# A mixture-of-experts kernel: six expert weight slots instead of four, and weight rows of 24 KB instead of three pieces of 8 KB

## The reference, cut to what matters

```python
scores = jax.nn.sigmoid(tf @ router_w)
_, idx = lax.top_k(scores + router_bias, TOP_K)            # 8 of 64
gate = ROUTED_SCALE * gate / jnp.sum(gate, -1, keepdims=True)
...
def expert_block(acc, blk):                                # a block: the slots of one expert
    tok, g, e = blk
    xb = t_ext[tok]
    hb = jax.nn.silu(xb @ w1[e]) * (xb @ w3[e])
    return acc.at[tok].add((hb @ w2[e]) * g[:, None]), None
...
shared = (jax.nn.silu(tf @ sw1) * (tf @ sw3)) @ sw2
return acc[:n_tok] + shared
```

## Time and profile before

| | |
|---|---|
| median of 3 runs | 2488.39 us (2487.3 to 2493.26) |
| the profiled execution | 2497.42 us |
| its span | 2495.5 us |
| mean granted clock of TensorE | 0.888 |
| PE busy | 1998.0 us (80%) |
| DMA, mean over the span | 241 GB/s |

### The profile page before, as it was taken

One profiled execution on the slowest core, in us unless ns is written; L12 is line 12 of the kernel. 1 busy time (PEld: TensorE's weight loads), 2 busy tenths in 40 slices (PEclk: granted clock), 3 DMA queues, 4 the chain that ended last, 5 costly groups with the idle time before them and its releaser, 6 DMA issues. The chain is left out here.

```text
span 2495.5 us, 31783 instructions
## 1 busy us (share of the span) xinstructions
PE 1998.0 (80%) x10528; PEld 1022.9 (41%) x10529; DVE 856.1 (34%) x1752; ACT 236.5 (9%) x517; POOL 678.0 (27%) x961
## 2 busy tenths in 40 slices
PE   4795679955778988899998986859768887787795
PEld 0343433333355544455454433324455444443442
DVE  0005710077545222233232353654352222222224
ACT  0102101122020000000000011011110000000001
POOL 0000000022003554466565400000005444344340
PEclk8896689967877999899999988979879999899898
DMA  9300067100224899988999565130247999999964
GB/s 390 160 1 1 5 243 270 59 1 1 89 82 168 346 410 402 402 343 337 372 357 399 239 286 227 52 135 34 89 192 303 399 415 399 396 394 392 402 277 171
DMA packets 99962, 601.47 MB, mean 241 GB/s; under 512 B 23200, under 2 KB 23435, under 8 KB 40444
## 3 DMA queue, kind: packets, MB, share of 16 engines
q1 hardware_dynamic: 66012, 516.78, 51.4%
q0 software_dynamic: 33888, 83.86, 9.0%
HBM read 590.50 MB, written 51.92 MB: 257 GB/s over the span
## 5 line engine op out<-in xcount | busy, mean ns | idle before, releaser
L1593 PE MATMUL bank<-moe_w,blk_xT 128*64 128x256 f32 x5632 | 701.1, 405 | 0.0
L1593 PEld LDWEIGHTS bank<-moe_w,blk_xT 128*64 128x64 f32 x5632 | 413.7, 146 | 230.6 <-issue 50.5
L1521 POOL DMA_INDIRECT blk_came<-v_tokens,blk_gidx x352 | 362.1, 1029 | 185.9 <-issue 180.5
L1667 DVE STREAM_TRANSPOSE blk_xT<-blk_came 128x512 f32<-128x512 f32 x176 | 125.3, 712 | 614.2 <-PE bank L1593 597.2
L1604 PE MATMUL bank<-moe_w,blk_hT 128*64 128x512 f32 x1408 | 332.0, 592 | 1.5 <-DVE blk_hT L1679 1.5
L450 PE MATMUL bank<-w_in_ring,xt 128*128 128x512 f32 x544 | 243.1, 607 | 12.5 <-DMA w_in_ring<-in_odd_w_in 9.7
L1537 POOL DMA_INDIRECT y_rows<-blk_y,blk_sidx x176 | 179.3, 1019 | 97.3 <-issue 48.4
L1686 DVE COPY blk_y<-bank 128x512 f32<-128x512 f32 x176 | 121.7, 692 | 149.3 <-PE bank L1604 149.3
L450 PEld LDWEIGHTS bank<-w_in_ring,xt 128*128 128x128 f32 x544 | 104.8, 194 | 148.5 <-issue 138.4
L1586 PE MATMUL bank<-base,blk_hidden 128*128 128x128 f32 x176 | 58.9, 335 | 132.6 <-DMA moe_w<-in_experts 130.5
L1650 ACT ACTIVATE blk_silu<-bank 128x128 f32<-128x128 f32 x174 | 48.2, 277 | 1112.2 <-PE bank L1593 1112.2
(11 more groups left out here) (381 smaller groups left out, 1652.5 us busy)
## 6 DMA issues: line engine op xcount, KB each, us to landing
moe_w<-in_experts SPq DMA_DIRECT2D x128, 3072.0 KB
ada_ring<-in_ada_w SPq DMA_DIRECT2D x12, 2048.0 KB, 16.4
w_out<-in_ada_w POOLq DMA_DIRECT2D x12, 2048.0 KB, 7.7
moe_w<-y_rows SPq DMA_DIRECT2D x24, 1024.0 KB, 18.9
w_in_ring<-in_even_w_in SPq DMA_DIRECT2D x8, 2048.0 KB, 11.7
w_in_ring<-in_odd_w_in SPq DMA_DIRECT2D x7, 2048.0 KB, 12.5
blk_came<-v_tokens,blk_gidx POOLq DMA_INDIRECT x352
w_out<-in_even_w_out SPq DMA_DIRECT2D x1, 4096.0 KB, 12.5
```

The source lines that it names most:

```text
L1521: pool.indirect_dma_start(came[:, q, u], None, v_quarters, bass.IndirectOffsetOnAxis(ap=gidx[q][:, u:u + 1], axis=0), bounds_check=4 * n_t ...
L1593: last = nc.tensor.matmul(g.bank[1][64 * h:64 * h + 64, 0:HID], xT[:, k], w[:, s, (2 * k + h) * HID:(2 * k + h + 1) * HID], start=k == 0, ...
L1667: nc.vector.transpose(xT[:].rearrange("p k (u t) -> p u k t", u=2), came[:, q].rearrange("p u (k t) -> p u k t", k=KT)).then_inc(xt_ready, 1)
```

## The change

`SLOTS` is 6 and `PIECE` is the whole row, so a weight load is 128 runs of 24 KB. The room for two more slots (48 KB a partition) comes from scratch tiles that now lie elsewhere: the router's tables in slots not yet loaded, `came` for three of four blocks in `ada_rows`, `y`, `silu`, `hidden`, `hT` and one half of `sh_hidden` in `xt`, and the rows, `z` and `sh_down` of the last stage in `w`. Three things move with that. `sh_down` is loaded at the start of `expert_residual_stage` instead of in `routing_stage`. `ada_columns_stage(g, 1)` runs in the even layer, ahead of `hgrn_stage`, since `ada_rows` is overwritten afterwards. `routing_stage` loads experts 0 to 3; expert 4 is loaded at the start of `blocks_stage` without a wait, expert 5 after `shared_up`. As 64 is no multiple of 6, the loops take ten turns of six, the first written out, and four more experts are written out behind. The ring of the last stage has 13 places instead of 10.

```diff
-SLOTS = 4
+SLOTS = 6
+WHOLE_TURNS, LAST_EXPERTS = EXPERTS // SLOTS, EXPERTS % SLOTS
...
-PIECE = 2 * D
+PIECE = WEXP
...
-    RING = 10
+    RING = 13
...
+                sp.dma_start(sh_down, g.dram["experts"][l * (EXPERTS + 1), 0, :, W13:WEXP]).then_inc(sh_down_loaded, 16)
                 for u in range(nt * PAIRS):
...
-                for s in range(SLOTS - 1):
+                for s in range(SLOTS - 2):
                     load_expert(sp, r["w"][:, s], experts[1 + s]).then_inc(r["expert_loaded"][s], 16)
-                load_expert(sp, r["sh_down"], experts[0, W13 // PIECE:]).then_inc(r["sh_down_loaded"], 16)
...
-        came, xT = sb("came", [P, DEPTH, 2, D // 4]), sb("xT", [P, KT, SB])
+        came = [g.ada_rows[:, q] for q in range(3)] + [sb("came", [P, D // 2])[:]]
...
+                load_expert(sp, w[:, SLOTS - 2], experts[SLOTS - 2]).then_inc(loaded[SLOTS - 2], 16)
                 sp.wait_ge(sh_up_done, 1)
                 load_expert(sp, w[:, SLOTS - 1], experts[SLOTS - 1]).then_inc(loaded[SLOTS - 1], 16)
-
-                with sp.Fori(1, EXPERTS // SLOTS) as turn:
+                with sp.Fori(1, WHOLE_TURNS) as turn:
                     for s in range(SLOTS):
...
+                        load(turn, s)
+                for s in range(LAST_EXPERTS):
+                    load(WHOLE_TURNS, s)
...
-                pool.memset(came[:], 0.0).then_inc(came_zeroed, 1)
-                pool.wait_ge(came_zeroed, 1)
+                for x in came:
+                    pool.memset(x, 0.0).then_inc(came_zeroed, 1)
+                pool.wait_ge(came_zeroed, DEPTH)
...
-                with pe.Fori(1, EXPERTS // SLOTS) as turns:
+                with pe.Fori(1, WHOLE_TURNS) as turns:
                     for s in range(SLOTS):
                         expert(turns, s)
+                for s in range(LAST_EXPERTS):
+                    expert(WHOLE_TURNS, s)
...
+            ada_columns_stage(g, 1)
             hgrn_stage(g, work, {"q": q[:], "v": v, "f": (ff[:], fb[:]), "y": y})
```

More of the change, by code:

```diff
@@ L1105, in expert_residual_stage @@
     diag = room[:, RING * 2 * D:RING * 2 * D + nt * BY_PE * P].rearrange("p (u c) -> p u c", c=P)
+    rest = room[:, RING * 2 * D + nt * BY_PE * P:]
+    sh_down, sh_down_loaded = rest[:, 0:2 * D], new_sem(g, "sh_down_loaded")
+    ln, z = (rest[:, (2 + 2 * i) * D:(4 + 2 * i) * D].rearrange("p (a d) -> p a d", a=2) for i in range(2))
     with ExitStack() as ctx:
         sb = lambda n, shape: ctx.enter_context(nc.sbuf_tensor(f"xln_{n}{l}", shape, F32))
-        ln, z, stats, mv = sb("rows", [P, 2, D]), sb("z", [P, 2, D]), sb("stats", [P, 2, 2, 6]), sb("mv", [P, 4, 4])
+        stats, mv = sb("stats", [P, 2, 2, 6]), sb("mv", [P, 4, 4])
         marks = {}
@@ L1134, in _ @@
                         for half in range(2):
-                            nc.tensor.matmul(g.bank[2 * n + half][:], r["sh_hidden"][:, m, n * P:(n + 1) * P],
-                                             r["sh_down"][:, m * D + half * 512:m * D + (half + 1) * 512], start=m == 0, stop=False)
+                            nc.tensor.matmul(g.bank[2 * n + half][:], r["sh_hidden"][m][:, n * P:(n + 1) * P],
+                                             sh_down[:, m * D + half * 512:m * D + (half + 1) * 512], start=m == 0, stop=False)
                     for k in range(BY_PE):
@@ L1311, in routing_stage @@
         chosen_f, lin, blk, slot, val = (sb(n, [P, nt, TOPK]) for n in ("chosen_f", "lin", "blk", "slot", "val"))
[L1312 to L1314 removed]
+        free, at = r["w"][:, SLOTS - 2], 0
+        tables = []
+        for shape in ((nt, TOPK, EXPERTS), (1, TOPK, EXPERTS), (2, TOPK, SB), (2, TOPK, NB)):
+            size = math.prod(shape)
+            tables.append(free[:, at:at + size].rearrange("p (a b c) -> p a b c", a=shape[0], b=shape[1]))
+            at += size
+        onehot, prod, in_slot, in_block = tables
+        prod = prod[:, 0]
+        rb, nblk, incl, start, odd = (free[:, at + i * EXPERTS:at + (i + 1) * EXPERTS] for i in range(5))
         ecol, val0 = sb("ecol", [P, 2]), sb("val0", [P, 1])
[L1316 to L1318 removed]
         flat = lambda t: t[:].rearrange("p n e -> p (n e)")
@@ L1339, in _ @@
                     dve.wait_ge(squashed, n + 1)
[L1340 removed]
+                    link(nc.vector.tensor_tensor(pick[:, n], sig[:, n], rb, ALU.add))
                     link(nc.vector.max(top[:, n], pick[:, n]))
@@ L1438, in _ @@
                 for u in range(3):
-                    last = nc.tensor.matmul(g.bank[2][:, u * NB:(u + 1) * NB], g.spread[:, u], listing[:], start=True, stop=True)
+                    last = nc.tensor.matmul(g.bank[2][:, u * NB:(u + 1) * NB], g.spread[:, u], listing, start=True, stop=True)
                 last.then_inc(laid, 1)
@@ L1585, in turn_hidden @@
                     pe.wait_ge(hidden_done, b + 1)
-                    nc.tensor.transpose(g.bank[2][:, 0:P], hidden[:], g.ident).then_inc(hid_turned, 1)
+                    nc.tensor.transpose(g.bank[2][:, 0:P], hidden, g.ident).then_inc(hid_turned, 1)
                 def up_project(b, s):
@@ L2180, in odd_layer @@
     nc = g.nc
-    ada_columns_stage(g, 1)
     allt, lat = list(range(NT)), [2, 3]
```

111 lines of the change are left out of this document (59 added, 52 removed).

## The result

The changed kernel takes 2523.7 us (median of 4 runs, 2521.53 to 2533.84), the kernel before on the same chip 2487.85 (2487.09 to 2493.26). The ratio is 1.0147, 95% interval 1.0116 to 1.0178: slower, where 2441 was forecast, and outside the range. The profiled execution has a span of 2532.0 us, 36.5 more than before.

A forecast was written before the change was run, and what follows sets the result against it. Layer 0 was taken as bound by DMA, then PE, then DMA again, layer 1 by saturated DMA. Terms of -33 (layer 0), -21 (layer 1), +5 and +2 (costs) gave -47 us: 2441 us from 2488.39, range 2412 to 2476.

The forecast's parts named there:

- the term for the rows: Weight loads in both layers: longer rows take 0.12 us off a load, 3 us in layer 0 and 7 in layer 1.
- rival 1: In the expert blocks, long weight rows hold up the gathers: a tail of 27 us, 2468 us; chance 0.13.
- The head start: Expert loads issued earlier: a lead of two loads, 16 us, in layer 0; 1.6 loads, 13.9 us, in layer 1.
- the slots: Two more weight slots: 7 us off the later waits in layer 0, nothing by itself in layer 1.
- beyond the waits: Layer 0 time lost besides PE's waits: a share of 13.7 us, of which half, 7 us, was counted as gained.
- The costs: Later `sh_down` load, 2.5 us in each layer, 5 us; first gathers and memsets, 2 us for both layers.
- the first gather: Layer 1's start: sharing engines with expert 4 delays it; 2 us with the memsets for both layers, between 0 and 6.
- Rival 2: PE's longer loop is fetched again at each jump back: up to 87 us, 2528 us; chance 0.05.
- rival 3: Both layers: the lead is worth less and rows bring nothing; -15 us, 2473 us; chance 0.10.
- rival 4: Layer 0 becomes wholly PE's and all its 59 us lost go; -73 us, 2415 us; chance 0.10.
- rival 5: Loads don't speed up: 24 KB rows move slower, say by 2%, with half the lead; about 2485 us; chance 0.05.
- sign of error: The prediction is wrong if PE still waits over 30 us in layer 0, or a layer 1 load takes 8.7 us or more.

## Why the prediction was wrong

**The failed step is the term for the rows, and rival 1, which should have priced it.** The sum counts the long rows as a gain of 10 us (3 in layer 0, 7 in layer 1) and puts their cost for q0 at nothing; measured, rows of 24 in place of 8 KB cost 67 us with six slots. The prediction knew the mechanism: rival 1 has the slowed small queue and even 9.9 us for a block. It got 0.13, because of two sentences. "Gathers run four blocks ahead" is true of the gathers, and DVE waited for no gather within the loops; but the scatter has less room. It is issued three blocks behind, and its `y` buffer is wanted again some 13 us later, about two and a half blocks. The wait fell on L1708, and the sign named for this rival, DVE waiting for `blk_came`, stayed away. "The loads run dry first and the engines stay busy" assumed that the engines' time is conserved. They did not. The first 500 us of layer 1's blocks, in the changed kernel and then with six slots and rows of 8 KB (columns as in the earlier trace rows):

```profile
1922.00:2422.00 500.00, 408.93 (x2700) 195.58 (x2702) 112.99 (x264) 18.33 (x66) 225.19 (x326) 0.92 0.94 388
```

```profile
1874.00:2374.00 500.00, 421.40 (x2871) 217.28 (x2871) 128.16 (x282) 19.43 (x70) 241.24 (x350) 0.94 0.99 395
```

The engines were 0.94 busy instead of 0.99; the better rate of long rows made up for part of that, and what they moved is 2% less, some 9 us. (The window 2000:2100 alone would not show it: 403 GB/s against 395 with rows of 8 KB.) The rest of the 21 us by which layer 1 differs lies in the tail, from the last load to the last hidden transpose. GB/s in 40 slices, windows 2420:2480 and 2350:2410:

```profile
GB/s 47 27 0 262 475 298 571 300 326 349 25 0 0 175 11 0 0 11 0 0 17 60 90 90 14 0 55 115 0 0 153 3 0 0 0 0 0 0 0 0
```

```profile
GB/s 411 404 341 418 412 429 434 402 431 410 432 423 391 415 415 413 440 252 156 64 23 0 41 63 0 0 0 169 0 0 0 156 0 0 0 0 0 0 0 0
```

The loads end near 2435 and near 2377 us: a tail of some 39 us against 27. The kernel before had some 27 too, so rival 1 had the kind of loss right that its tail names, and in layer 1 it grew by 12. In layer 0, where PE had been the bound for a part, a block of 8 to 10 us in place of 5.58 costs directly: 55 us (629.4 against 574.3). Rival 1's price was a tail of 27 us on the forecast; the rows cost 67 (2523.7 against 2456.6), mostly as slow blocks all through layer 0.

The prediction's rule that each packet of q0 lets one of q1 pass fits the slowest blocks, 9.54 and 10.29 us apart. As a mean it is too hard. At 1.53 packets of q0 to one of q1, at least a third of them passed with no packet of q1 between, and the mean block took 629.4 / 99 = 6.4 us in layer 0 and 551.3 / 75 = 7.35 us in layer 1, not 9.9. The Trainium skill (DMA: Bandwidth & Descriptors, section "Queues, rings and completion order") has the round between queues go packet by packet; that the waits grow with the length of the other queue's packets agrees with it, the mean block does not show a strict one for one, and no profile view shows the order on one engine itself.

**The head start and the slots: right.** Measured apart, with rows of 8 KB, layer 0 got 37 us shorter (611.5 to 574.3) and layer 1 20 (550.2 to 530.0). The sum had 33 and 21, with 3 and 7 of it from the rows; without them 30 and 14. PE's waits for weights in layer 0 fell from 38.8 to 16.4 us, 22.4 where 26 less the rows' 3 was said. The other 15 of the 37 us went beyond the waits, where the prediction had halved 13.7 to 7. In layer 1 the lead is 1.54 loads by the prediction's own figures and not 1.6, which is half a microsecond.

**The row size: right in rate, wrong as a gain.** 418 against 404 GB/s at full share is more than assumed, and none of it reached the end.

**The costs: right but for the first gather.** In the changed kernel DVE's first add came 29.98 us after the last hidden transpose in layer 0, before 27.50; in layer 1 23.59, before 21.17. That is 2.5 and 2.4 us for the predicted 2.5. Layer 1's first gather, priced at 2 us together with the memsets, is worse: from the router's first matmul to the first hidden transpose 51.26 us, before 44.33, so 6.9. With rows of 8 KB it is 5.6, and 1.0 with expert 4 held back. The bound of 6 had been near, and a value in the lower half was chosen.

**Rival 2** named 2528 us, close to what came, for a reason that did not occur. Window 930:1420 of the changed kernel, within the loops of layer 0:

```profile
q8 instruction: 1, 0.02, 0.0%
```

One packet, not eight jumps' worth; in layer 1 none comes between 2060 and 2410. The turn of six experts is fetched once a layer.

**Rivals 3, 4 and 5** did not occur; rival 5 had slower loads, and they were faster. What was named as a sign of error (PE waiting over 30 us for weights in layer 0, a slow load) did not see this outcome either: PE waited for no expert's weights at all.

## What to carry to other kernels

When one queue's transfers get longer pieces, work out for every other queue on the same engines how many packets it needs per unit of work, and what they take if each lets one packet of the big queue pass. Compare that with the time per unit of work: here all was well at 3.5 us for a block of 5.8, nearly so at 5.3, and 1.3% (four slots) to 2.7% (six) of the whole time were lost at 10. Ask of each buffer that the small queue fills or frees how many units ahead its transfer is issued; the shortest such lead, not the longest, meets the delay first. And when a rival's arithmetic gives a rate below the stage's own, price it over the whole stage, unless a row shows who makes up for it.

## What the runs showed of the hardware that was not expected

A row of 24 KB goes as one packet, which holds its engine for some 0.94 us. Beside gathers and scatters the loads' rate at full share still grows with the row, from 384 GB/s at 4 KB over 404 at 8 KB to 418 at 24 KB. What it costs the other queue: a scatter's median time from issue to landing is 12.7 us in layer 0 and 19.6 in layer 1, where it is 7.1 and 7.0 beside rows of 8 KB.
